# Another order of the work behind the recurrence of a hybrid attention block

## The reference

```python
o = recurrence(q, k, v, beta, g)                              # 4 chunks of 64
o_dn = rmsnorm(o, dn_norm) * silu(z)
score = sum_h iw[h] * relu(iq[h] @ ik.T)   # 8 index heads, block-causal
admitted = top 64 of score, for each query
o_sa = softmax(sq @ sk.T where admitted) @ sv
o_xa = softmax(xq @ mk.T) @ mv,  mk, mv = rmsnorm(mem) @ w_mem_kv
x = x + (gates of o_dn, o_sa, o_xa) @ w_out;  x = x + ffn(x)
```

## Time and profile before

| | |
|---|---|
| median of 3 runs | 3981.64 us (3976.42 to 3982.71) |
| the profiled execution | 3987.29 us |
| its span | 3985.3 us |
| TensorE busy | 3752.7 us, 94% of the span |
| VectorE busy | 2318.2 us, 58% |
| ScalarE busy | 1775.4 us, 45% |
| DMA from HBM | 653.92 MB, 164 GB/s over the span |

### The profile page before, as it was taken

The page is one execution under the profiler, slowest core; times in us unless marked ns, Lnnn a source line. Parts: engine busy times, 40 slices in busy tenths (PEclk is TensorE's granted clock), DMA queues, the critical chain, the costliest instruction groups (busy, mean ns, idle before and its releaser), DMA issues.

```text
span 3985.3 us, 62822 instructions
## 1 busy us (share of the span) xinstructions
PE 3752.7 (94%) x23922; PEld 3202.1 (80%) x23922; DVE 2318.2 (58%) x3659; ACT 1775.4 (45%) x2628; POOL 8.4 (0%) x16
## 2 busy tenths in 40 slices
PE   8999999999999999999688999999899999999998
PEld 7977779999987688999456999985787877776655
DVE  7565535656656554665445556533555555688887
ACT  6522344434542245343224344333344444577775
POOL 0000000000000000000000000000000000000000
PEclk9999999999999899999898999999899999999998
DMA  5431455454441344555110555531255555699996
GB/s 200 137 112 54 147 163 173 155 183 156 150 153 50 111 164 158 176 184 175 54 52 27 166 183 174 184 114 51 89 185 173 184 172 185 215 332 338 337 334 250
DMA packets 181883, 657.67 MB, mean 165 GB/s; under 512 B 20208, under 2 KB 22256, under 8 KB 181056
## 3 DMA queue, kind: packets, MB, share of 16 engines
q1 hardware_dynamic: 180576, 648.39, 48.6%
q0 software_dynamic: 1120, 6.67, 0.5%
HBM read 653.92 MB, written 1.05 MB: 164 GB/s over the span
## 4 chain that ended last, share of the span: by engine, by line
PE 87%; DVE 9%; ACT 2%; issue 2%; DMA 0%; DVEq 0%; POOL 0%; ACTq 0%; SPq 0%
PE bank L765 14%; PE bank L766 14%; PE bank L767 14%; PE bank L1126 5%; PE bank L1128 5%; PE bank L1127 5%; PE bank L1633 4%; PE bank L383 3%; PE bank L1150 3%; PE bank L1151 3%; PE bank L1152 3%; PE bank L590 1%; PE bank L348 1%; DVE moe_w_low L1249 1%; PE bank L611 1%
## 5 line engine op out<-in xcount | busy, mean ns | idle before, releaser
L1249 DVE TENSOR_TENSOR moe_w_low<-ring,moe_w_high 128x1024 fp32r<-128x1024 f32 x528 | 640.1, 1224 | 262.9 <-ACT moe_w_high L1189 254.7
L1189 ACT ACTIVATE moe_w_high<-ring 128x1024 fp32r<-128x1024 f32 x528 | 556.0, 1060 | 331.8 <-PE bank L1128 218.9
L802 DVE TENSOR_TENSOR gates_w_low<-ring,gates_w_high 128x1024 fp32r<-128x1024 f32 x244 | 297.7, 1223 | 224.2 <-ACT gates_w_high L787 224.2
L1126 PE MATMUL bank<-moe_w_high,picked_high 128*128 128x512 f32 (+4 forms) x968 | 390.8, 404 | 26.0 <-DVE moe_w_low L1249 26.0
L1128 PE MATMUL bank<-moe_w_high,picked_low 128*128 128x512 f32 (+4 forms) x968 | 383.7, 396 | 0.0
L1127 PE MATMUL bank<-moe_w_low,picked_high 128*128 128x512 f32 (+4 forms) x968 | 383.0, 396 | 0.0
L787 ACT ACTIVATE gates_w_high<-ring 128x1024 fp32r<-128x1024 f32 x244 | 257.0, 1056 | 253.1 <-PE bank L767 253.1
L765 PE MATMUL bank<-first_x_high,first_w_high 128*128 128x256 f32 x848 | 246.5, 291 | 1.3 <-DVE first_w_low L802 1.1
L766 PE MATMUL bank<-first_x_high,first_w_low 128*128 128x256 f32 x848 | 244.2, 288 | 0.0
L767 PE MATMUL bank<-first_x_low,first_w_high 128*128 128x256 f32 x848 | 243.8, 287 | 0.0
L1126 PEld LDWEIGHTS bank<-moe_w_high,picked_high 128*128 128x128 f32 (+4 forms) x968 | 164.9, 170 | 89.1 <-DVE moe_w_low L1249 32.3
(11 more groups left out here) (479 smaller groups left out, 9481.1 us busy)
## 6 DMA issues: line engine op xcount, KB each, us to landing
ring<-in_moe SPq DMA_DIRECT2D x528, 512.0 KB, 4.9
ring<-in_w_in SPq DMA_DIRECT2D x186, 512.0 KB, 3.4
ring<-in_w_ffn SPq DMA_DIRECT2D x132, 512.0 KB, 3.3
ring<-in_even_ffn SPq DMA_DIRECT2D x132, 512.0 KB, 3.3
ring<-in_mod_w SPq DMA_DIRECT2D x96, 512.0 KB, 3.4
ring<-in_w_branch SPq DMA_DIRECT2D x48, 512.0 KB, 3.4
ring<-in_w_mem SPq DMA_DIRECT2D x32, 512.0 KB, 3.4
ring<-in_even_in SPq DMA_DIRECT2D x20, 512.0 KB, 3.3
```

The lines of the kernel that those rows point to most:

```text
L802: subtract(low[:, s % 3, :], ring[:, g % RING, :], high[:, s % 3, :], ALU.subtract)\
L1126: mm(out, xh, wh, start=i == 0, stop=False)
L1189: nc.scalar.activation(high[:, (s0 + q) % 3, :], ring[:, (g0 + q) % RING, :], ACT.Copy).then_inc(c.sem("high_ready"), 1)
L1249: tt(low[:, (s0 + q) % 3, :], ring[:, (g0 + q) % RING, :], high[:, (s0 + q) % 3, :], ALU.subtract)\
```

## The change

Only the order changes; no instruction is added or taken away, and the stream of slabs stays as it is.

- TensorE: the scores of block 0 and two of the four banks of value transposes come ahead of the head sums; the other two banks come between sums and spread; the scores of block 1 come behind the spread.
- ScalarE: the relus of block 0 come right behind the squares, ahead of the root. The 8 raw_high of memory move behind the copies of values. The 5 rows are no longer together: one is ahead of the relus of block 1, one behind memory's squares, and one behind each of the high parts of memory's slabs 0, 1 and 2. Memory's squares come ahead of the high parts.
- VectorE: the additions of block 0 come ahead of the reciprocal; the 8 raw_low of memory come behind the product with silu(z), ahead of the additions of block 1. A wait of VectorE for its own product goes.

```diff
 TensorE
-                pe.wait_ge(*c.at("squared", ("o2", l)))
-                token_sums(te, k, ("o2", l), sq8, DNH, NP2)
-                for j in range(4):
-                    ... transposes of bank j
-                token_spread(te, k, ("o2", l), nrm, DNH, NP2, 2)
-                pe.wait_ge(*c.at("index_rope", l))
-                for p in range(NP2):
-                    ... scores of block p
+                pe.wait_ge(*c.at("index_rope", l))
+                scores(0)
+                for j in range(2):
+                    sparse_values(j)
+                pe.wait_ge(*c.at("squared", ("o2", l)))
+                token_sums(te, k, ("o2", l), sq8, DNH, NP2)
+                for j in range(2, 4):
+                    sparse_values(j)
+                token_spread(te, k, ("o2", l), nrm, DNH, NP2, 2)
+                scores(1)
                 some_mods(l, MODS_IN[0] - mod_next[l])
 ScalarE
                 mem_high = round_high(sc, stream, f"mem{l}", ring, mem_w[0])
-                for i in range(KT):
-                    raw_high(sc, ("mem", l), memn, ...)
+                relus(0)
                 token_root(sc, ("o2", l), nrm, 32, 1.0 / P)
                 for j in range(4):
                     ... copy of transposed values, bank j
-                for p in range(NP2):
-                    ... relus of block p
-                mod_rows(MODS_IN[0] - 10)
-                for q in range(3):
-                    mem_high(q, 0)
+                for i in range(KT):
+                    raw_high(sc, ("mem", l), memn, ...)
+                mod_rows(1)
+                relus(1)
                 for j in range(4):
                     ins = af(sq8[:, 2 * j:2 * j + 2, :], memn[:, 2 * j:2 * j + 2, :], ACT.Square)
                 ins.then_inc(*sc.count("squared", ("mem", l)))
+                mod_rows(1)
+                for q in range(3):
+                    mem_high(q, 0)
+                    mod_rows(1)
 VectorE
-                for i in range(KT):
-                    raw_low(ve, ("mem", l), memn, ...)
+                scored(0)
                 token_inverse(ve, ("o2", l), nrm, 32)
                 ... output times gain, inverse root and silu(z)
-                dve.wait_ge(*ve.last())
-                for p in range(NP2):
-                    ... additions of block p
+                for i in range(KT):
+                    raw_low(ve, ("mem", l), memn, ...)
+                scored(1)
```

More of the change, by code:

```diff
@@ L1806, in _, with scores, sparse_values @@
                     last.then_inc(*te.filled(("o", l, ch)))
-                pe.wait_ge(*c.at("squared", ("o2", l)))
-                token_sums(te, k, ("o2", l), sq8, DNH, NP2)
-                for j in range(4):
+                def scores(p):
+                    for j in range(4):
+                        pe.wait_ge(*te.take(("score", l, p, j)))
+                        ps = te.bank
+                        r = slice(64 * (j % 2), 64 * (j % 2) + 64)
+                        for i in range(2):
+                            last = mm(ps[:, i * T:i * T + P * (p + 1)], Bq[r, 24 + 2 * (j // 2) + i, p * P:(p + 1) * P], ixk[r, 0:P * (p + 1)], start=True, stop=True)
+                        last.then_inc(*te.filled(("score", l, p, j)))
+                def sparse_values(j):
                     kt, h0 = j // 2, 4 * (j % 2)
@@ L2159, in _, with relus @@
                 mem_high = round_high(sc, stream, f"mem{l}", ring, mem_w[0])
-                for i in range(KT):
[L2161 to L2168, removed]
-                for p in range(NP2):
+                def relus(p):
                     for j in range(4):
@@ L2178, in _ @@
                         af(relu[:, n % 2, :, 0:nk], src, ACT.Relu).then_inc(*sc.emptied(("score", l, p, j)))
-                mod_rows(MODS_IN[0] - 10)
-                for q in range(3):
-                    mem_high(q, 0)
+                relus(0)
+                token_root(sc, ("o2", l), nrm, 32, 1.0 / P)
+                for j in range(4):
+                    kt, h0 = j // 2, 4 * (j % 2)
+                    act.wait_ge(*c.full(("svt", l, j)))
+                    ps = c.bank(("svt", l, j))
+                    af(vtok[:, kt, h0 * P:(h0 + 4) * P], ps[:, :], ACT.Copy).then_inc(*sc.emptied(("svt", l, j)))
+                for i in range(KT):
+                    raw_high(sc, ("mem", l), memn, v["norm_mem"][:, 8 * l:8 * l + 8], mem_x[0], i, c.at("mem_loaded", l))
+                mod_rows(1)
+                relus(1)
                 for j in range(4):
@@ L2184, in _ @@
                 ins.then_inc(*sc.count("squared", ("mem", l)))
+                mod_rows(1)
+                for q in range(3):
+                    mem_high(q, 0)
+                    mod_rows(1)
+                assert mods_read == MOD_GROUPS * l + MODS_IN[0]
                 for q in range(3, 16):
@@ L2609, in _, with scored @@
                         rope_step(j)
-                for i in range(KT):
-                    raw_low(ve, ("mem", l), memn, v["norm_mem"][:, 8 * l:8 * l + 8], mem_x[0], mem_x[1], i)
+                def scored(p):
+                    nk = P * (p + 1)
+                    for j in range(4):
+                        dve.wait_ge(*c.empty(("score", l, p, j)))
+                        for i in range(2):
+                            h = 2 * (2 * (j // 2) + i) + j % 2
+                            prev = k["admit"][:, P * p:P * p + nk] if h == 0 else score[p][:, 0:nk]
+                            dve.wait_ge(*ve.last())
+                            stt(out=score[p][:, 0:nk], in0=relu[:, (4 * p + j) % 2, i, 0:nk], scalar=iw[:, 8 * p + h:8 * p + h + 1],
+                                        in1=prev, op0=ALU.mult, op1=ALU.add).then_inc(*ve.count("scored", (l, 4 * p + j)))
+                scored(0)
                 token_inverse(ve, ("o2", l), nrm, 32)
@@ L2622, in _ @@
                 tt(A[:, 24:32, :], A[:, 24:32, :], o, ALU.mult).then_inc(*ve.count("dn_done", l))
-                dve.wait_ge(*ve.last())
-                for p in range(NP2):
[L2627 to L2635, removed]
+                for i in range(KT):
+                    raw_low(ve, ("mem", l), memn, v["norm_mem"][:, 8 * l:8 * l + 8], mem_x[0], mem_x[1], i)
+                scored(1)
                 mem_low = round_low(ve, stream, f"mem{l}", ring, mem_w, tt)
```

## The result

The changed kernel takes 3961.12 us (median of 4 runs, 3955.72 to 3964.21), the kernel before 3982.18: ratio 0.9948, interval 0.9932 to 0.9964, so 21 us less. The forecast was 3970.8, 10.8 less, and its range ended at 3962.5. The sign was right and the size half. The profiled execution took 3964.21 (span 3962.2), against 3987.29 before. One execution of a later kernel (after_delay30) took 16576 us, and its ratio leaves it out.

A forecast was written before the change was run, and what follows sets the result against it. TensorE was taken as the bound, losing time to gaps and lower clock behind the recurrence. Per layer 7.0 - (24.2 - 21.14) + 1.5 = 5.4, counted twice 10.8, from 3981.64 to 3970.8 us; range 3962.5 to 3979.5.

The forecast's parts named there:

- Part 1: From the recurrence's end to the first group's row: reordering fills TensorE's gap, and the row is copied 7.0 us earlier.
- the lead: How much earlier the first group's row is copied: 411.7 instead of 418.73, 7.0 us, bounds 4.5 to 8.4.
- rival C: Head sums stay slow because the clock stays at 0.50: lead 4.5, 2.9 us a layer, 3975.8; chance 0.25.
- Part 2: From the first group's row to memory's first product: 24.2 us instead of 21.14, the price of the new order.
- Both new gaps: TensorE waits for rows before the third and fourth groups, 2.1 and 3.6 us, each followed by the lower clock.
- the 2.1 gap: TensorE's wait before the third group, behind relus and memory's squares; a clock fall assumed although shorter than earlier gaps.
- Part 3: At memory's start: the slow stretch of 3.10 at clock 0.50 goes, winning 1.5 us a layer.
- Rival B: Behind the recurrence the clock holds: sums at 3.73, no fall behind the new gaps, 9.4 us a layer, 3962.8; chance 0.15.

The follow-up runs named there:

- after_delay30: The changed kernel with 30 dense products, whose results nobody reads, added once in layer 1 behind the sparse attention: 3972.8 us, ratio 0.998 to the kernel before.
- rows_early: The changed kernel with the second row copied ahead of memory's squares, the third ahead of mem_high(0), the fourth ahead of mem_high(1): 3947.6 us, ratio 0.9916.
- before_again: The kernel before, unchanged, measured against itself as a null test: 3979.29 us, ratio 0.9993.

## Why the prediction was wrong

**Part 1 held in layer 0 and not in layer 1.** TensorE still stands 0.66 ahead of the sums (0.6 forecast), 8 transposes took 1.09 (0.9), scores(1) 2.10 (1.9). In layer 0 the first group's row is copied at 410.53 instead of 418.73; 0.6 of these 8.2 came before the stretch, so the lead is 7.6, 7.0 forecast. The forecast has the sums at 4.24; they took 3.73, and the spread paid with 5.26 at the lower clock. In layer 1 the sums took 5.79, the transposes behind them 1.95 and the spread 5.73, all slow. From the end of the recurrence to the transpose behind the first group it took 22.0 there (1319.86, which is 1319.59 + 0.27, to 1341.87) against 26.4 before (1330.84 to 1357.20): a lead of 4.4, which is rival C's 4.5. So the 7.0 did not count twice: part 1 gave 12.0 of the 14.0. All four profiles of the changed kernel have this split, 3.73 in layer 0 and 5.78 to 6.04 in layer 1. Why the same order has another clock in the second layer no run shows.

The Trainium skill ("TensorE: Matmul & The Clock Gate", Part 4, on PE-mode transpose) has it that transposes don't engage the full clock. Here 8 of them took 1.09 behind dense work, full clock, and the sums behind them 3.73 in one layer and 5.79 in the other: the rule can't be told right or wrong by these two, and rival C, which hung beside it, was right in layer 1 only.

**Part 2 was too dear.** Both new gaps came in both layers, from the causes named, in layer 0 at 1.82 (2.1) and 3.02 (3.6), the slab landing in 3.3 (3.9: 418.37 to 421.71). But I let the clock fall behind both. It fell behind one in each layer: behind the 3.02 in layer 0 (4.95), behind the 1.82 in layer 1 (5.28), with 3.62 behind the other. From the row to memory it took 22.0 in layer 0 and 22.2 in layer 1, not 24.2, which gives back 4.2 of the 6.1 that part 2 was to cost. I called the 2.1 gap the weak point because it is the shorter. In layer 1 the fall stood behind the shorter gap in two profiles (this one and after_delay30's) and behind the longer in the other two, so the length does not decide it. What all four profiles have is one fall a layer and not two.

**Part 3 held**: no gap, and 1.00 at memory's start. Together: 8.1 and 4.7 in the two layers, 12.8 for 10.8. That these are so near is in part luck: part 2 gave 4.2 more than forecast and part 1 gave 2.0 less. rows_early, without the two gaps, shows what they cost: 7.5 in its stretch and 12 in the runs.

**The step that failed** is one sentence on bounds and what I made of it: "Behind memory's start TensorE has no gap, so its start time passes on to all that follows", with each gain counted twice and nothing else moving. The start does pass on: the lead of 8.8 behind memory's first 48 products of layer 0 is still 8.8 when the kernel before is at 600 us. But what follows does not keep its length. By the runs, another 8 to 9 us, clock alone, came from places that no edit touches, and the sum had them at nothing.

How sure is this surplus of the runs over the stretch? Every kernel with the new order or a part of it has it: 7 to 13 us in eight comparisons, the changed kernel's two among them, and 6.0 to 14.2 in the four with a delay, when the added work is allowed for. The seven comparisons of the old order, null test, fills and delays, have -0.9 to 5.2. One comparison's interval is some 5 us either way, so the two groups show it and no single kernel does. The 20 profiles show less: outside the stretch and the delays the eight of the old order took 3859.1 us on average and the twelve with the new order or a part of it 3855.5, with standard errors of 2.5 and 1.2. The first pair of profiles, 3869.2 and 3859.1, lies 10 apart.

That the surplus goes with the new order is shown by the runs; why is not, and the cause stays open. It isn't the shift (after_delay30 keeps it), and a mark of single profiles, the router region (4.6 in the first pair), doesn't follow it. Rival B's number, 3962.8, was the nearest, but not its mechanism, since the clock fell in both layers.

## What to carry to other kernels

The copy of a row, or any small result that TensorE waits for, goes ahead of whatever waits for a DMA or another engine on the same in-order queue; that was worth 12 us here. Price a gap of TensorE as its length plus what the clock may lose behind it (6.4 us a layer here for gaps of 8.4). A fall is not certain behind each gap, and which gap it takes can change from one execution to the next, but the sum over the stretch hardly did here. Two layers with the same instructions can still pay differently (8.1 and 4.7), so read both before a gain is counted twice. When a change moves gaps, a forecast to 10 us of 4000 has to allow for the clock in code that isn't touched, and a single profile should not be read for it.

## What the runs showed of the hardware

- The same 32 instructions behind the same 0.66 gap took 3.73 (layer 0 of the changed kernel) or 6.06 (layer 0 of rows_early); the instructions ahead of them were the same too.
- Ahead of the change nothing differs, and yet the recurrence of layer 0 ends at 392.41 in one profile of the kernel before and at 387.13 in the other (before_again). Of the 5.3 between them, 5.1 is the lower clock:
```profile
385.13 2.00 PE L1805 MATMUL bank<-arena 64*128 64x64 f32 x16
```
- The kernel before ran from 3965.94 to 3991.5 in one set of 16 runs.
